# Gated delta rule of an encoder layer: 16-row blocks inverted by substitution, one block per partition, in place of three doubling levels

## The chip, the cores and the metric

The kernel runs on one core of one Trainium2 chip. TensorE is called PE here, VectorE DVE, ScalarE ACT, GpSimd POOL and SyncE SP. The metric is the device time of one execution in microseconds (us); of several executions the median counts.

## The reference

One layer of an encoder over 2048 tokens of width 1024, all in float32: an input projection, two groups of heads (gated delta rule and latent attention), an output projection, a feed-forward network and a gated embedding, with norms between. Only the delta rule concerns this change. For each of 4 heads (key and value width 128) and each chunk of 64 tokens:

```python
g = jnp.cumsum(chunks(g), axis=-1)
decay = jnp.exp(jnp.where(tri_incl, g[..., :, None] - g[..., None, :], -jnp.inf))
k_beta = k * beta[..., None]
lower = jnp.where(tri_strict, jnp.einsum('nbhid,nbhjd->nbhij', k_beta, k) * decay, 0.0)
rhs = jnp.concatenate([v * beta[..., None], k_beta * jnp.exp(g)[..., None]], -1)
sol = lax.linalg.triangular_solve(lower + jnp.eye(CHUNK), rhs, left_side=True, lower=True, unit_diagonal=True)
u, w = sol[..., :DV], sol[..., DV:]
attn = jnp.where(tri_incl, jnp.einsum('nbhid,nbhjd->nbhij', q, k) * decay, 0.0)
...
v_new = u_c - jnp.einsum('bhck,bhkv->bhcv', w_c, state)
o = jnp.einsum('bhck,bhkv->bhcv', q_c, state) + jnp.einsum('bhij,bhjv->bhiv', attn_c, v_new)
state = state * jnp.exp(gl)[..., None, None] + jnp.einsum('bhck,bhcv->bhkv', k_c, v_new)
```

q and k are normed to length one per head beforehand; o gets a root-mean-square norm, a gain and a gate z.

## The kernel before

`build` (L2643) calls eight stages one after the other, each with its own buffers and semaphores and a barrier at its end: `project_in`, `latents`, `delta_rule`, `attention`, `project_norm`, `feed_in`, `project_norm`, `embed`. Stages exchange tensors through HBM. The change is in `delta_rule` (L625) alone, and in the two scratch tensors that `build` now makes for it.

`delta_rule` works on 16 tiles of 128 tokens, two chunks each, all four heads together, so most instructions work on 128 partitions by 512 elements (4 heads by 128). There are three jobs for a tile:

- **first**: load q, k, v (768 KB, names `dr_qkv`), transpose them on PE, take sums of squares on ACT (`p_squares`), roots and one Newton step (`p_newton`), scale q and k (`p_scale`, `dr_qk_n`), transpose them back (`p_back`), products of k with k and of q with k (`p_gram`), masks of decays on POOL (`masks`, `dr_dec`), from which DVE makes the triangle L (`p_grams`, L1232), whose transpose gives the first U (`p_turn_l`, `p_inverse`).
- **solve**: the inverse U of 1+L, by five doubling levels of sizes 2, 4, 8, 16, 32. A level is `s_z` on PE (transposes of U L939, products of L and U L941), a copy T on ACT (L1116), a masked copy Z on DVE (L1247), `s_y` on PE (L948) and a subtraction on DVE (`s_u`, L1252). Then `s_wu` makes w and u.
- **advance**: twice per tile, a chunk's step of the state S: `a_state` (L974, L978) and `a_update` (L986, L989) on PE, `a_v` (L1257) and `a_s` (L1268) on DVE, with a scaled state `Sd` from POOL (L853); then `a_squares`, `a_norm` (L1272 to L1279), a transpose `a_out` and `a_gate` (L1285), which writes `dr_mix`, stored by SP.

The order is written out by hand for each engine in a function `all_three`: one round holds the advance of tile t, the solve of tile t+1 and the first job of tile t+2, interleaved. `pipeline` runs 14 such rounds in hardware loops of two, with a filling round ahead and two emptying ones behind. Engines meet by semaphores only, and each engine takes its instructions strictly in the order written. SP's queue holds the loads of q, k, v (four tiles ahead, two buffers), of z, and the stores of `mix`.

Of the kernel before, what the change touches and what calls it, by code (L numbers as in the profile page):

```python
# [24 lines left out]
ACT = mybir.ActivationFunctionType  # L25
# [599 lines left out]
def delta_rule(nc, hT, a_log, dt_bias, norm_g, mixT):  # L625
# [5 lines left out]


    LEVELS = (2, 4, 8, 16, 32)
    BETA, GCUM, BETA_G, K_DEC, GATE = range(5)
    with ExitStack() as ctx:
        s = Scope(nc, ctx, "dr")
        qkv = s.sb("qkv", [P, 2, 3 * HEADS, P])
# [8 lines left out]
        cur = s.sb("cur", [P, 2, 5, HEADS])  # L646
# [5 lines left out]
        corner = s.sb("corner", [P, 1 + len(LEVELS), P])  # L652
        eps_l2 = s.sb("eps_l2", [P, 1])
        cums = s.sb("cums", [P, HEADS, P])
        eg = s.sb("eg", [P, 2, HEADS, P])
        e_last = s.sb("e_last", [P, HEADS, 2])
# [3 lines left out]
        qk_n = s.sb("qk_n", [P, 2 * HEADS, P])  # L660
        vb = s.sb("vb", [P, 2, HEADS, P])
        kbg = s.sb("kbg", [P, 2, HEADS, P])
        kdec = s.sb("kdec", [P, 2, HEADS, P])
        qk_nT = s.sb("qk_nT", [P, 2 * HEADS, P])
        dif = s.sb("dif", [P, HEADS, P])
        dec = s.sb("dec", [P, 2, HEADS, P])
        L = s.sb("L", [P, 2, HEADS, P])
        Z = s.sb("Z", [P, HEADS, P])
        Z0 = s.sb("Z0", [P, HEADS, P])
        U = s.sb("U", [P, 2, HEADS, P])  # L670
        T = s.sb("T", [P, HEADS, P])
        attnT = s.sb("attnT", [P, 2, HEADS, P])
        wT = s.sb("wT", [P, 2, HEADS, P])
        u = s.sb("u", [P, 2, HEADS, P])
        qdT = s.sb("qdT", [P, 2, HEADS, P])
        S = s.sb("S", [P, HEADS, P])
        Sd = s.sb("Sd", [P, HEADS, P])
# [5 lines left out]
        mix = s.sb("mix", [P, HEADS, P])  # L683
# [5 lines left out]
        loaded = [s.sem(f"loaded{b}") for b in range(2)]  # L689
        z_loaded = [s.sem(f"z_loaded{b}") for b in range(2)]  # L690
        cur_done = s.sem("cur_done")
        cums_done = s.sem("cums_done")
        qk_turned = s.sem("qk_turned")
        turned_done = s.sem("turned_done")
        eg_done = s.sem("eg_done")
        ssq_done, log_done, root_done = s.sem("ssq_done"), s.sem("log_done"), s.sem("root_done")
        newton = s.sem("newton")
        scaled = s.sem("scaled")
        vb_done = s.sem("vb_done")
        dif_done, dec_done = s.sem("dif_done"), s.sem("dec_done")  # L700
        kbg_done, kdec_done = s.sem("kbg_done"), s.sem("kdec_done")
        masked = s.sem("masked")
        back_done, back_copied = s.sem("back_done"), s.sem("back_copied")
        gram_done = s.sem("gram_done")
        L_done, attn_done = s.sem("L_done"), s.sem("attn_done")
        LT_done, z0_done, u_done = s.sem("LT_done"), s.sem("z0_done"), s.sem("u_done")

# [3 lines left out]
        qd_done = s.sem("qd_done")  # L711
        last_done = s.sem("last_done")
# [5 lines left out]
        NL = len(LEVELS)  # L718
        PAIR = [slice(0, 2), slice(2, 4)]
        solve_ps = [solve0, solve1]  # L720
        N_MASKS = 5 + 2 * (1 + NL) + 1
        PRE_GATE = 13

        def column(c):
# [1970 lines left out]
```

## Time and profile before

| what | us |
|---|---|
| median of 3 runs (3538.44 to 3544.13) | 3541.79 |
| the profiled execution, its own time | 3540.79 |
| its span, first to last instruction | 3539.3 |
| `delta_rule`: first mask instruction to the end of the last `dr_mix` | 705.4 to 1207.2 |

The page lists for each group of instructions the line, the engine, the operation, the names written and read, the count, the busy time, the mean duration of one, and the idle time of the engine ahead of them with what ended it. The timeline lists instructions in order of time: start, length, engine, line, and in brackets the idle time before and its releaser. A table by stretches gives, for each stretch from start to end, its length, the busy time and count for PE, PE's weight loads, DVE, ACT and POOL, then the granted PE clock as a share of 2.4 GHz, the share of the DMA engines' time and the GB/s. A float32 matmul counts as two instructions of PE, a transpose as one.

### The profile page before, as it was taken

Reading aid. Unit: us, or ns where it says so; the run is one execution under the profiler, and the core shown is the slowest. Engines: PE = TensorE matmul, PEld = TensorE weight load, DVE = VectorE, ACT = ScalarE, POOL = GpSimd, SP = SyncE. Lnnn points to the kernel's source line nnn. Section 1 sums busy time; section 2 is a strip of 40 time slices with the busy share of each in tenths; the row PEclk is TensorE's granted clock in tenths of the full one; section 3 lists DMA queues with packets and bytes.
Section 4 is the critical chain, followed back from the end, with each engine's and each line's share of the span. In section 5 each row is a group of like instructions: output and inputs, shape, how many; then the busy total and the mean of one; then the engine's idle time right before and its main releaser. Section 6 shows DMA issues by size and latency. Waiting matters only on the chain. (4 is left out here: it accounts for less than half of the span.)

```text
span 3539.3 us, 48206 instructions
## 1 busy us (share of the span) xinstructions
PE 3218.3 (91%) x16244; PEld 2679.7 (76%) x16244; DVE 1689.5 (48%) x2776; ACT 1131.5 (32%) x2514; POOL 1037.2 (29%) x863
## 2 busy tenths in 40 slices
PE   7999987779999689796997999989999799999798
PEld 5888864568888577685875888878888588888576
DVE  3652004346666555554567554585555433333433
ACT  2111014334444355454224333343333311111321
POOL 2222212033333176652006333363333100000222
PEclk9999998989999899998998999999999899999899
DMA  3212124311111311102553322212222533333433
GB/s 137 77 71 83 71 97 129 118 54 48 45 52 28 84 57 43 53 21 94 176 168 137 123 78 89 79 64 89 78 82 65 190 101 97 97 93 98 161 120 105
DMA packets 263069, 323.20 MB, mean 91 GB/s; under 512 B 15152, under 2 KB 205616, under 8 KB 258480
## 3 DMA queue, kind: packets, MB, share of 16 engines
q1 hardware_dynamic: 211544, 239.09, 21.2%
q0 software_dynamic: 18144, 66.07, 5.2%
q10 hardware_dynamic: 33280, 16.78, 1.7%
q8 instruction: 53, 0.87, 0.1%
q14 instruction: 48, 0.39, 0.0%
HBM read 209.68 MB, written 112.20 MB: 91 GB/s over the span
## 5 line engine op out<-in xcount | busy, mean ns | idle before, releaser
L1942 PE MATMUL ff_bank<-ff_x_hi,ff_w_lo 128*128 128x512 f32 x1240 | 489.1, 394 | 34.3 <-DVE ff_w_lo L2122 19.7
L1943 PE MATMUL ff_bank<-ff_x_lo,ff_w_hi 128*128 128x512 f32 x1240 | 488.0, 394 | 0.0
L1944 PE MATMUL ff_bank<-ff_x_hi,ff_w_hi 128*128 128x512 f32 x1240 | 487.6, 393 | 0.0
L1925 POOL TENSOR_TENSOR ff_w_sum<-ff_w_raw 128x512 f32<-128x512 f32 x210 | 294.3, 1411 | 504.3 <-DVE ff_w_lo L2122 443.3
L1942 PEld LDWEIGHTS ff_bank<-ff_x_hi,ff_w_lo 128*128 128x128 f32 x1240 | 236.0, 190 | 86.7 <-DVE ff_w_lo L2122 22.8
L2322 PE MATMUL fd_acc<-fd_w_hi,fd_a_lo 128*128 128x512 f32 x704 | 278.0, 395 | 25.4 <-DVE fd_a_lo L2306 25.4
L176 PE MATMUL in_h_ps<-in_x_hi,in_w_lo 128*128 128x512 f32 x704 | 276.8, 393 | 25.5 <-POOL in_w_lo L153 25.5
L177 PE MATMUL in_h_ps<-in_x_lo,in_w_hi 128*128 128x512 f32 x704 | 276.2, 392 | 0.0
L178 PE MATMUL in_h_ps<-in_x_hi,in_w_hi 128*128 128x512 f32 x704 | 276.2, 392 | 0.0
L2324 PE MATMUL fd_acc<-fd_w_hi,fd_a_hi 128*128 128x512 f32 x704 | 275.8, 392 | 0.0
L2323 PE MATMUL fd_acc<-fd_w_lo,fd_a_hi 128*128 128x512 f32 x704 | 275.8, 392 | 0.0
L1944 PEld LDWEIGHTS ff_bank<-ff_x_hi,ff_w_hi 128*128 128x128 f32 x1240 | 236.1, 190 | 49.5
L1943 PEld LDWEIGHTS ff_bank<-ff_x_lo,ff_w_hi 128*128 128x128 f32 x1240 | 236.1, 190 | 48.8
L2021 ACT ACTIVATE ff_w_hi<-ff_w_sum 128x512 fp32r<-128x512 f32 x210 | 132.6, 631 | 285.7 <-PE ff_bank L1944 266.3
L2306 DVE TENSOR_TENSOR fd_a_lo<-fd_a_raw,fd_a_hi 128x256 fp32r<-128x256 f32 x176 | 74.6, 424 | 277.8 <-ACT fd_a_hi L2296 277.8
L2296 ACT ACTIVATE fd_a_hi<-fd_a_raw 128x256 fp32r<-128x256 f32 x176 | 73.1, 416 | 346.3 <-PE fd_acc L2324 338.7
L1502 POOL TENSOR_TENSOR at_prob<-at_prob,at_scale 128x512 f32<-128x512 f32 (+4 forms) x112 | 133.6, 1223 | 158.6 <-DVE at_scale L1688 98.9
L2322 PEld LDWEIGHTS fd_acc<-fd_w_hi,fd_a_lo 128*128 128x128 f32 x704 | 133.2, 189 | 56.2 <-DVE fd_w_lo L2303 26.6
L176 PEld LDWEIGHTS in_h_ps<-in_x_hi,in_w_lo 128*128 128x128 f32 x704 | 133.5, 190 | 54.4 <-issue 17.3
L178 PEld LDWEIGHTS in_h_ps<-in_x_hi,in_w_hi 128*128 128x128 f32 x704 | 133.4, 189 | 28.0
L177 PEld LDWEIGHTS in_h_ps<-in_x_lo,in_w_hi 128*128 128x128 f32 x704 | 133.5, 190 | 27.7
L2324 PEld LDWEIGHTS fd_acc<-fd_w_hi,fd_a_hi 128*128 128x128 f32 x704 | 133.1, 189 | 28.0
(368 smaller groups left out, 6858.4 us busy)
## 6 DMA issues: line engine op xcount, KB each, us to landing
ff_w_raw<-w_gate_up SPq DMA_DIRECT2D x44, 1024.0 KB, 5.2
scratch_hT<-in_out SPq DMA_DIRECT2D x22, 1024.0 KB, 3.8
fd_a_raw<-scratch_hid SPq DMA_DIRECT2D x176, 128.0 KB, 2.1
dr_qkv<-scratch_hT SPq DMA_DIRECT2D x16, 768.0 KB, 5.0
in_w_raw<-w_in POOLq DMA_DIRECT2D x22, 512.0 KB, 3.8
scratch_hid<-ff_first SPq DMA_DIRECT2D x44, 256.0 KB, 2.3
scratch_hid<-ff_second SPq DMA_DIRECT2D x44, 256.0 KB, 2.3
in_x_raw<-xT SPq DMA_DIRECT2D x8, 1024.0 KB, 4.8
```

Source lines behind the costliest of these rows:

```text
L176: pe.matmul(acc, w_lo[:, b, ws], x_hi[:, k, ts], start=(k == 0), stop=False)
L177: pe.matmul(acc, w_hi[:, b, ws], x_lo[:, k, ts], start=False, stop=False)
L178: last = pe.matmul(acc, w_hi[:, b, ws], x_hi[:, k, ts], start=False, stop=(k == KD - 1))
L1502: op = pool.tensor_tensor(view, view, by, ALU.mult)
L1925: pool.tensor_tensor(w_sum[:, SUM_SLOT[m]], w_raw[:, b, one], w_raw[:, b, two], op).then_inc(w_sum_done, 1)
L1942: pe.matmul(acc, w_lo[:, wm, ws], x_hi[:, xm, k], start=first_mm, stop=False, skip_group_check=skip)
L1943: pe.matmul(acc, w_hi[:, wm, ws], x_lo[:, xm, k], start=False, stop=False, skip_group_check=skip)
L1944: return pe.matmul(acc, w_hi[:, wm, ws], x_hi[:, xm, k], start=False, stop=last_mm, skip_group_check=skip)
L2021: act.activation(w_hi[:, m], src, ACT.Copy).then_inc(w_hi_done, 1)
L2322: pe.matmul(to, self.a_lo[:, slot, rows], self.w_hi[:, k, cols], start=(k == k0), stop=False)
L2323: pe.matmul(to, self.a_hi[:, slot, rows], self.w_lo[:, k, cols], start=False, stop=False)
L2324: last = pe.matmul(to, self.a_hi[:, slot, rows], self.w_hi[:, k, cols], start=False, stop=(k == k1))
```

## The change

`delta_rule` is written anew. The parts, in words:

- **No norming of q and k.** The products are made from `dr_qkv` as loaded; the norms go into factors per row (`p_factors`, `made`, `rnq`). `p_scale`, `p_back`, both copies back and the transposes of L are gone. `kdec` and `kbg` move from POOL to DVE, the state's scaling joins DVE's addition (four instructions of one head each in place of one on POOL and one on DVE).
- **Blocks of 16 rows.** Levels 2, 4 and 8 (and the size-1 start) are gone. Instead SP stores L to HBM (256 KB), loads its 32 diagonal blocks of 16 by 16 back with one block in each of 32 partitions (four loads of 128 pieces of 64 bytes), POOL inverts them in 29 instructions (`substitute`), SP stores the result (32 KB), loads it back spread over 128 partitions (512 pieces of 64 bytes), and DVE puts the blocks on U's diagonal (`spread`). Levels 16 and 32 stay.
- **Four tiles in flight.** A round r holds the first job of tile r, the substitution of tile r-1, the solve of r-2 and the advance of r-3. There are 19 rounds, written out without hardware loops. Buffers grow: `qkv` 3, `eg`, `kdec`, `attnT`, `qdT` 4, `L`, `kbg`, `vb` 3, `mix` 2.

```diff
-    LEVELS = (2, 4, 8, 16, 32)
+    BASE = 16
+    NB = P // BASE
+    LEVELS = (16, 32)
...
+            for r in range(TILES + 3):
+                m, e, n, t = (x if 0 <= x < TILES else None for x in (r, r - 1, r - 2, r - 3))
+                yield m, e, n, t
...
+            for m, e, n, t in steps():
+                if e is not None:
+                    sp.wait_ge(inv_step, INV * (e + 1))
+                    sp.dma_start(blocks_U[e], inv[:, e % 2].rearrange("p j i -> p (j i)")).then_inc(inv_stored, 16)
+                    if e + 3 < TILES:
...
+                        load(e + 3)
+                    sp.wait_ge(inv_stored, 16 * (e + 1))
+                    reached(sp, u_done, e - 1)
+                    src = blocks_U[e].rearrange("(h r) (j i) -> (r j) h i", h=HEADS, j=BASE)
+                    sp.dma_start(u_blk[:, e % 2], src).then_inc(u_loaded[e % 2], 16)
+                if m is not None:
+                    sp.wait_ge(L_done, m + 1)
+                    sp.dma_start(blocks_L[m], L[:, m % 3].rearrange("p h f -> p (h f)")).then_inc(L_stored, 16)
+                    sp.wait_ge(L_stored, 16 * (m + 1))
+                    reached(sp, inv_step, INV * (m - 1))
+                    row = HEADS * P
+                    for h in range(HEADS):
+                        src = bass.AP(blocks_L.tensor, blocks_L[m].offset + h * P,
+                                      [[BASE * row + BASE, NB], [row, BASE], [1, BASE]])
+                        sp.dma_start(blk[h * NB:(h + 1) * NB, m % 2], src).then_inc(blk_loaded[m % 2], 16)
...
+            def substitute(e):
...
+                pool.wait_ge(blk_loaded[b], 16 * HEADS * (e // 2 + 1))
+                reached(pool, inv_stored, 16 * (e - 1))
+                low = blk[:, b].rearrange("p i j -> p j i")
+                pool.tensor_tensor(inv[:, b], ident_b[:], low, ALU.subtract).then_inc(inv_step, 1)
+                for k in range(1, BASE - 1):
+                    shape = [HEADS * NB, k, BASE - 1 - k]
+                    by = blk[:, b, k + 1:, k].unsqueeze(1).broadcast_to(shape)
+                    row = inv[:, b, 0:k, k:k + 1].broadcast_to(shape)
+                    to = part[:, 0:shape[1] * shape[2]].rearrange("p (j i) -> p j i", j=k)
+                    rest = inv[:, b, 0:k, k + 1:]
+                    pool.wait_ge(inv_step, n + 2 * k - 1)
+                    pool.tensor_tensor(to, by, row, ALU.mult).then_inc(inv_step, 1)
+                    pool.wait_ge(inv_step, n + 2 * k)
+                    pool.tensor_tensor(rest, rest, to, ALU.subtract).then_inc(inv_step, 1)
...
+            for m, e, n, t in steps():
+                if m is not None:
+                    sums(m)
+                if e is not None:
+                    substitute(e)
+                if m is not None:
+                    decayed(m)
+                    masks(m)
...
+            def p_lower(m):
+                dve.wait_ge(gram_done, m + 1)
+                dve.wait_ge(masked, 3 * m + 3)
...
+                dve.tensor_tensor(L[:, m % 3], b0[:], dec[:, 0], ALU.mult).then_inc(L_done, 1)
...
+            def spread(e):
+
+                shape = [P, HEADS, NB, BASE]
+                dve.wait_ge(u_loaded[e % 2], 16 * (e // 2 + 1))
...
+                dve.tensor_tensor(U[:, e % 2].rearrange("p h (r i) -> p h r i", i=BASE),
+                                  u_blk[:, e % 2].unsqueeze(2).broadcast_to(shape),
+                                  diag[:].rearrange("p (r i) -> p r i", i=BASE).unsqueeze(1).broadcast_to(shape),
+                                  ALU.mult).then_inc(u_done, 1)
```

The order on POOL, one round in the middle of the stage, before (`dr_Sd` is the scaled state, `dr_dec` the masks):

```order
L826 TENSOR_TENSOR dr_cums<-dr_upto,dr_cur 128x512
L85 REGISTER_ALU
L853 TENSOR_TENSOR dr_Sd<-dr_S,dr_e_last 128x512
L852 REGISTER_ALU
L853 TENSOR_TENSOR dr_Sd<-dr_S,dr_e_last 128x512
L831 TENSOR_TENSOR dr_dec<-dr_dif,dr_below 128x512
```

and now, the end of the substitution of tile r-1 (`dr_part` and `dr_inv`; 24 rows of the same kind stand ahead of these) and what follows it for tile r:

```order
L843 TENSOR_TENSOR dr_part<-dr_blk,dr_inv 32x26
L845 TENSOR_TENSOR dr_inv<-dr_inv,dr_part 32x13x2
L843 TENSOR_TENSOR dr_part<-dr_blk,dr_inv 32x14
L845 TENSOR_TENSOR dr_inv<-dr_inv,dr_part 32x14
L860 TENSOR_TENSOR dr_qdT<-dr_qkv,dr_eg 128x512
L850 TENSOR_TENSOR dr_dec<-dr_dif,dr_upto 128x512
L852 TENSOR_TENSOR dr_dec<-dr_dif,dr_below 128x512
L855 TENSOR_TENSOR dr_dec<-dr_dec,dr_made 128x512
L827 TENSOR_TENSOR dr_cums<-dr_upto,dr_scal 128x512
```

The masks of tile r stand behind the whole substitution of tile r-1, where before only two scalings of the state stood ahead of them.

The order on SP's queue, one round in the middle of the stage, before:

```order
L752 DMA dr_qkv<-scratch_hT 128x12x128
L763 REGISTER_ALU
L764 ISA
L764 DMA scratch_mixT<-dr_mix 128x4x128
L756 ISA
L756 DMA dr_zT<-scratch_hT 128x4x128
```

and now (`blocks_L` and `blocks_U` are the new scratch tensors in HBM):

```order
L762 DMA scratch_blocks_U<-dr_inv 32x256
L745 DMA dr_qkv<-scratch_hT 128x12x128
L771 DMA dr_u_blk<-scratch_blocks_U 128x4x16
L774 DMA scratch_blocks_L<-dr_L 128x512
L781 DMA dr_blk<-scratch_blocks_L 8x16x16 x4
L785 DMA scratch_mixT<-dr_mix 128x4x128
L749 DMA dr_zT<-scratch_hT 128x4x128
```

The load of q, k, v now stands between the store of the inverted blocks and their load back, and L's store and the blocks' loads follow on the same queue.

The order on DVE, the end of a round, before (from the norm of the output to the end of the round):

```order
L1279 TENSOR_TENSOR dr_on<-dr_b,dr_orn 128x512
L1252 TENSOR_TENSOR dr_U<-dr_U,dr_b 128x256 x2
L1228 ISA
L85 ISA
L1232 TENSOR_TENSOR dr_L<-dr_b,dr_dec 128x512
L1246 REGISTER_ALU
L1247 TENSOR_TENSOR dr_Z<-dr_b,dr_corner 128x256 x2
L1235 TENSOR_TENSOR dr_attnT<-dr_b,dr_dec 128x512
L1252 TENSOR_TENSOR dr_U<-dr_U,dr_b 128x256 x2
```

and now:

```order
L1206 TENSOR_TENSOR dr_U<-dr_u_blk,dr_diag 128x512
L1243 TENSOR_TENSOR dr_orn<-dr_orn 128x4
L1244 TENSOR_SCALAR dr_ossq<-dr_ossq 128x4
L1246 TENSOR_TENSOR dr_orn<-dr_orn,dr_ossq 128x4
L1248 SCALAR_TENSOR_TENSOR dr_orn<-dr_orn 128x4
L1250 TENSOR_TENSOR dr_orn<-dr_orn,dr_rnq 128x4
L1253 TENSOR_TENSOR dr_on<-dr_b,dr_orn 128x512
L1193 TENSOR_TENSOR dr_L<-dr_b,dr_dec 128x512
L1198 TENSOR_TENSOR dr_attnT<-dr_b,dr_dec 128x512
L1259 SCALAR_TENSOR_TENSOR dr_mix<-dr_b,dr_gnorm,dr_zT 128x512
```

L of tile r now stands behind the instruction that reads the loaded blocks of tile r-1 (L1206) and behind the norm of tile r-3.

## Rows read from the trace of the kernel before

**Rows 1.** Busy time by stretch: us, busy per engine, clock, DMA, GB/s.
```profile
786.40:1190.00 403.60, 397.21 (x3164) 357.11 (x3162) 257.01 (x590) 182.11 (x728) 131.22 (x119) 1.00 0.14 40
```

**Rows 2.** The same view, one steady tile.
```profile
977.71:1006.48 28.77, 28.36 (x229) 25.52 (x227) 18.38 (x43) 13.44 (x55) 9.94 (x10) 1.00 0.16 46
```

**Rows 3.** Timeline, POOL's first mask in two tiles: start, us, engine, line.
```profile
977.71 1.27 POOL L831 TENSOR_TENSOR dr_dec<-dr_dif,dr_below 128x512 f32<-128x512 f32 x1 [2.02 <-ACT dr_dif L1098]
...
1006.48 1.27 POOL L831 TENSOR_TENSOR dr_dec<-dr_dif,dr_below 128x512 f32<-128x512 f32 x1 [2.02 <-ACT dr_dif L1098]
```

**Rows 4.** Timeline of PE in that tile: a level, then transposes back.
```profile
978.08 1.16 PE L948 MATMUL dr_b<-dr_Z,dr_T 128*128 128x128 f32 x8
...
979.31 0.44 PE L939 MATMUL dr_b<-dr_ident,dr_U 128*128 128x128 f32 x2
...
980.79 1.16 PE L986 MATMUL dr_b<-dr_vnew,dr_kdec 64*128 64x128 f32 x8
...
982.93 1.09 PE L879 MATMUL dr_b<-dr_ident,dr_qk_n 128*128 128x128 f32 x8
```

**Rows 5.** Groups by shape, POOL: count, busy us, mean ns, idle before.
```profile
L1502 POOL TENSOR_TENSOR at_prob<-at_prob,at_scale 128x512 f32<-128x512 f32 x32 | 33.1, 1040 | 23.7 <-DVE at_scale L1688 23.7
...
L1502 POOL TENSOR_TENSOR at_prob<-at_prob,at_scale 128x128 f32<-128x128 f32 x16 | 6.4, 400 | 44.7 <-DVE at_scale L1668 44.7
...
L834 POOL TENSOR_TENSOR dr_dec<-dr_dif,dr_upto 128x512 f32<-128x512 f32 x16 | 20.4, 1275 | 0.0
...
L804 POOL MEMSET dr_eps_l<- 128x1 f32 x1 | 0.1, 98 | 0.0
```

**Rows 6.** The timeline of POOL and SP in the stage's set-up.
```profile
705.76 0.66 SPq L771 DMA_DIRECT2D dr_bias<-dt_bias  x1
...
706.47 0.42 SPq L772 DMA_DIRECT2D dr_rate<-a_log  x1
...
706.93 0.43 SPq L773 DMA_DIRECT2D dr_gnorm<-gdn_norm_g  x1
...
708.43 0.66 POOL L798 TENSOR_SCALAR_AFFINE_SELECT dr_corner<-dr_ones 128x64 f32<-128x64 f32 x1
...
713.13 0.25 POOL L798 TENSOR_SCALAR_AFFINE_SELECT dr_corner<-dr_ones 128x64 f32<-128x64 f32 x1
...
713.44 0.24 POOL L798 TENSOR_SCALAR_AFFINE_SELECT dr_corner<-dr_corner 128x64 f32<-128x64 f32 x1
```

**Rows 7.** DMA issues by line: size of each, median us from issue to landing.
```profile
dr_qkv<-scratch_hT SPq DMA_DIRECT2D x16, 768.0 KB, 5.0
...
scratch_mixT<-dr_mix SPq DMA_DIRECT2D x16, 256.0 KB, 2.4
...
scratch_mixT<-at_out SPq DMA_DIRECT2D x32, 128.0 KB, 1.9
...
dr_bias<-dt_bias SPq DMA_DIRECT2D x1, 2.0 KB, 2.5
```

**Rows 8.** The view of one tensor, zT: last line, all its loads.
```profile
DMA to landing us min/median/max: 2.8/2.8/8.0
```

**Rows 9.** The timeline of the last tile, and the first tile's L.
```profile
1194.06 1.06 PE L974 MATMUL dr_b<-dr_S,dr_wT 128*64 128x128 f32 x8 [0.79 <-issue]
...
1203.86 0.16 DVE L1272 TENSOR_TENSOR dr_orn<-dr_orn 128x4 f32<-128x4 f32 x1 [1.99 <-ACT dr_orn L1135]
...
1204.53 0.69 DVE L1279 TENSOR_TENSOR dr_on<-dr_b,dr_orn 128x512 f32<-128x512 f32 x1
...
1206.42 0.75 DVE L1285 SCALAR_TENSOR_TENSOR dr_mix<-dr_b,dr_gnorm,dr_zT 128x512 f32<-128x512 f32 x1 [1.21 <-PE dr_b L879]
...
736.46 0.69 DVE L1232 TENSOR_TENSOR dr_L<-dr_b,dr_dec 128x512 f32<-128x512 f32 x1 [6.90 <-PE dr_b L920]
```

**Rows 10.** PE around a long idle, then the clock of that stretch.
```profile
751.19 1.97 PE L879 MATMUL dr_b<-dr_ident,dr_qk_n 128*128 128x128 f32 x8 [3.42 <-DVE dr_qk_n L1224]
...
752.00:756.00 4.00, 4.00 (x21) 4.00 (x20) 0.84 (x2) 1.09 (x2) 1.92 (x2) 0.50 0.00 0
```

More of the change, by code:

```diff
@@ L773, in _ @@
             sp.dma_start(gnorm[:], norm_g).then_inc(small_loaded, 16)
[L774 removed]
+            for t in range(3):
+                load(t)
             for t in range(2):
[L776 to L784 removed]
@@ L813, in _ @@
             put(below[:], chunk[:], ALU.is_gt, 0.0, 0, [[-1, P]], 1)
[L814 removed]
+            for l, size in enumerate(LEVELS):
                 blocks = P // (2 * size)
@@ L864, in all_three @@
-            def all_three(t, b, has_first=True, has_advance=True):
-                if has_first:
-                    sums(t + 2, b)
-                if has_advance:
-                    advance(t, b)
-                if has_first:
-                    masks(t + 2, b)
-                    products(t + 2, b)
-            pipeline(first, advance, all_three)(pool.Fori)
+            by_block = lambda ap: ap.rearrange("p (n r) -> p n r", r=BASE)
+            put(by_block(diag[:]), by_block(ones[:]), ALU.is_ge, 0.0, 0, [[-BASE, NB], [0, BASE]], 1)
@@ L875, in _, with transposes @@
         @block.tensor
         def _(pe):
-            def transposes(out, src, n0, count):
-                for h in range(count):
+            def transposes(out, src, n0):
+                for h in range(HEADS):
                     last = pe.transpose(out[:, h], src[:, n0 + h], ident[:])
@@ L1340, in _ @@
-            pre_scalars()
-            pipeline(first, advance, all_three)(dve.Fori)
+                dve.wait_ge(z_loaded[t % 2], 16 * (t // 2 + 1))
+                reached(dve, stored[t % 2], 16 * (t // 2))
+                dve.scalar_tensor_tensor(mix[:, t % 2], b2[:], gnorm[:, 0:1], zT[:, t % 2], ALU.mult, ALU.mult).then_inc(mix_done, 1)
+            pre_scalars()
+            for m, e, n, t in steps():
+                first, base, solve, advance = (x is not None for x in (m, e, n, t))
+                if advance:
+                    a_v(t, 0)
+                if solve:
+                    s_z(n, 0)
+                if advance:
+                    a_s(t, 0)
+                    a_v(t, 1)
+                if solve:
+                    s_u(n, 0)
+                if advance:
+                    a_s(t, 1)
+                if first:
+                    p_kdec(m)
+                    p_newton(m)
+                    p_factors(m)
+                    p_kbg(m)
+                if solve:
+                    s_z(n, 1)
+                    s_u(n, 1)
+                if base:
+                    spread(e)
+                if advance:
+                    a_norm(t)
+                if first:
+                    p_lower(m)
+                    p_attention(m)
+                if advance:
+                    a_gate(t)
```

700 lines of the change are left out of this document (297 added, 403 removed).

## The prediction

> **What bounds the kernel now.** I read the table by stretches first, to find the stage and who is busy in it. In the steady part of `delta_rule`, 403.6 us, PE is busy for 397.2 of it at the full clock of 2.4 GHz (share 1.00) [rows 1]. DVE has 257, ACT 182, POOL 131. Then one round: POOL's first mask starts at 977.71 and again at 1006.48, so a tile takes **28.77 us** [rows 3], of which PE is busy 28.36, DVE 18.4, ACT 13.4, POOL 9.9 [rows 2]. So the stage is bound by PE's work, 14 rounds of 28.8 us, with about 60 us of filling and emptying. The other stages are not touched: the whole change is what becomes of the time from 720 to 1207.2, where the last `dr_mix` ends [rows 9].
>
> **PE's side of the change.** A level's `s_y` starts at 978.08, its `s_z` at 979.31, the next group at 980.79: 2.71 us, of which I count some 0.25 between the two as waiting: 2.45 of work [rows 4]. Three levels go: 7.3 us. The eight transposes back are listed with 1.09 us, 0.9 without the overlap at their end, and four transposes of L with half of it [rows 4]. So 28.4 - 7.3 - 0.9 - 0.5 = **19.7 us of PE work** for a tile. The pieces left wait for one another somewhat more (a state step has the vector instruction between its two products, and fewer level pieces stand between); I put 2 us on it, so PE alone would allow a round of about 22. DVE: the levels' Z and U go, `kdec`, `kbg`, the spread and small factors come, the sum stays under 18.4. ACT loses copies. If nothing else entered, 14 rounds would each be 6.7 us shorter, 94 us in all. The question is what the new chain allows.
>
> **The new chain, step by step.** I follow it from the end of DVE's L of tile r to the end of L of tile r+1; both in the same place of a round, so this is the round's length if the chain binds. It is a closed loop, since SP, POOL and DVE each take their instructions in order: L(r) must go to HBM and back before POOL can substitute, and the masks and L of tile r+1 stand behind that on POOL and on DVE. The deeper buffers don't open this loop.
>
> 1. SP picks up (0.1 us, an estimate) and stores L, 256 KB. `mix` of the same size lands in 2.4 us [rows 7]. At 2.5.
> 2. Four loads of 64-byte pieces. SP issued small DMAs 0.71 and 0.46 us apart [rows 6]; three spacings of 0.5 and a landing of 2.5 for the last, as the broadcast of 128 small pieces took [rows 7], plus a pick-up: 4.1. At 6.6, POOL starts at 6.7.
> 3. `substitute`. POOL took 400 ns for 128 elements and 1040 for 512 with one broadcast operand [rows 5]: 1.67 ns for an element, 187 ns fixed; with two full operands 1275 for 512, 2.1 ns an element. The 28 small instructions have 14 to 56 elements, 40 in the mean (560 for each of two kinds, by 14): 0.26 us. A dependent instruction started 0.06 us behind its predecessor's end (713.13 + 0.25 to 713.44), I take 0.07. Short runs: 64 runs of one element took 0.66 us where two runs of 32 took 0.25 [rows 6], 6.6 ns a run for another kind of instruction; with 7.5 runs in the mean I take half of it, 0.025. So 28 x 0.355 = 9.9, and 0.8 for the first (256 elements): **10.7 us**. At 17.4. Bounds: below, every small one as cheap as the fill of one element, 0.098 [rows 5], plus the gap: 28 x 0.17 + 0.7 = 5.5; above, 0.400 as the nearest full row, plus gap and runs: 28 x 0.47 + 0.8 = 14.0. I stay between, since the line through the rows has them at 0.26.
> 4. The inverse is stored, 32 KB: 128 KB took 1.9, 256 KB 2.4 [rows 7]; 2.1 with a pick-up of 0.1. At 19.6. Meanwhile SP issues the next load of q, k, v at about 17.9; such a load lands after 5.0 us [rows 7], so at 22.9.
> 5. The blocks come back, issued at 19.7. Alone they would land after 2.5, at 22.2. But they stand behind 768 KB in the same queue. One load of z, alone 2.8 us, took 8.0 when it was issued behind two such loads [rows 8]. I take 0.8 us behind the big load's end: at 23.7. Bounds: 22.2 without queueing, 24.7 if such small pieces took 5.0 in all, as long as the 768 KB load [rows 7].
> 6. DVE: the spread 0.7, five small instructions of the norm and the product `on`. Before, four small ones took 1203.86 to 1204.53, and `on` 0.69 [rows 9]: 0.87 + 0.69. Then L, 0.69 [rows 9]. With a pick-up: 3.0. **At 26.7.**
>
> The other branch from step 3 goes through POOL's four big instructions (`qdT` and both plain masks 1.27 each, the last 1.04 [rows 5]): 17.4 + 4.9 + 0.7 = 23.0. It ends earlier. PE's branch ends at about 22. So the queue branch sets the round: 26.7 against 28.8. What PE saved is then mostly idle time: about 5 us of each round.
>
> [...]
>
> **Both ends of the stage.** The mask set-up has 12 instructions instead of 18, at 0.24 to 0.66 each [rows 6], about 2.5 us less. The first L ends at 737.15 [rows 9]; without scaling, transposes back and copies the first tile saves about another 4.7 us: 730. Then 15 rounds to L(15): rounds 1 and 2 have no norm (1.5 less each), rounds 14 and 15 no load in the queue (1.5 less each), so 4 x 25.2 + 11 x 26.7 = 394.5, at 1124.5. Then the last blocks (23), norm and gate of tile 13 (3): 1150.5. A round with only solve and advance: two levels 4.9, two state steps about 8, w and u with copies 3.3, some waits: 17. The last advance took 13.1 us before (1194.06 to 1207.17 [rows 9]); the output product now stands ahead of the second state product, 14.5. Cold PE, below: 3. End at 1185, against 1207.2: **22 us less**. The profiled execution had 3540.8, 1 us under the median, which is within the runs' spread: 3541.8 - 22 = **3520 us**. One us on the round is 14 us of the time. Idle PE costs speed when it comes back: after 3.42 us idle the eight transposes took 1.97 us instead of 1.09, and the clock was 0.50, the 1.2 GHz level, for the next 4 us [rows 10, 4]. With 5 us idle in each round the first 4 us of PE's work would take some 3 us longer; 22 + 3 = 25 is still under 26.7, so hidden, but the cover is only 1.7 us.
>
> **Rivals.**
> - **The chain is shorter, PE binds** (20%). POOL's small instructions cost under 0.29 us, or the queueing of step 5 isn't there (-1.5). The round then falls to 22 to 25: 3455 to 3496. For: the fill of one element takes 0.098. Against: nothing that reads two operands was seen that short.
> - **POOL's small instructions are dear; slower** (25%). At 0.42 us each, 0.065 more than taken, the round is 28.5 and the gain is gone; at 0.47 it is 30.0 and the time 3520 + 46 = 3566. Dearer 64-byte pieces (two loads on the chain, 1 us each) do the same. From a round of 28.6 the kernel is slower by over 0.2%. For: 64 short runs took 0.66. The place to see it is `substitute`.
> - **A wash** (12%): the same chain at 27.6 to 28.6, by 0.03 to 0.06 us per small instruction, 3535 to 3549.
> - **PE's clock opens the loop again** (3%): the first part of each round at 1.2 GHz makes PE's branch longer than the chain, 29 and more, 3555. Against: 25 by the rows above, and a shorter idle heals itself. The Trainium skill, "TensorE: Matmul & The Clock Gate", section "HAM oscillation", has PE return to the slow level after idle stretches between bursts; rows 10 show it once.
> - **Forecast** (40%): the queue branch binds at 25.2 to 27.6, 3499 to 3534.
>
> **How the numbers follow.** 0.2% of this kernel, 7 us, is about what a measurement can tell from no change. Faster: 40 + 20 and a little of the rest, 0.61. Same 0.12, slower 0.27. The range takes in the cheap case down to a round of 22.7 (3464) and the dear one up to 30.5 (3573).
>
> **What would show it.** Distance between two `dr_L` 26.7 us; `substitute` 10.7 us from first to last; DVE's instruction L1206 waiting for the DMA of `dr_u_blk`, not for POOL; PE busy about 20 of each 27 us, with one idle stretch before the output's transposes, and a clock under 1.00 in the steady part. Wrong if the masks (POOL) release L, if PE has no such gap, or if `dr_u_blk` lands in 2.5 us behind the load.

## The result, and the profile after

The changed kernel takes **3491.5 us** (median of 4 runs, 3487.7 to 3493.2) against 3541.5 before (3538.4 to 3544.1): ratio 0.9855, 95% interval 0.9841 to 0.9868. It is faster by 50 us, where 22 had been forecast. The direction and the chain that binds were as predicted, the size of the gain was not: the transfers on the chain land sooner than the prediction took. The profiled execution has a span of 3490.0 us, against 3539.3 before.

The table by stretches, in the steady part of `delta_rule` (columns as in [rows 1]):

```profile
778.30:1062.40 284.10, 245.43 (x1775) 212.56 (x1775) 152.05 (x440) 120.47 (x531) 162.88 (x404) 0.92 0.25 66
972.29:995.95 23.66, 21.11 (x154) 18.37 (x154) 12.94 (x39) 10.52 (x46) 13.98 (x34) 0.93 0.27 72
```

The second line is nearly one round. PE is busy for 86% of the stretch where it had 98% [rows 1], and its clock is 0.92 where it had 1.00. A round, from one `dr_L` to the next, takes 22.4 to 26.1 us, 24.13 in the mean of all 15; before, the round of [rows 3] took 28.8. The stage's last `mix` starts at 1149.4, where it had 1206.4 [rows 9].

I follow the loop of the prediction from L at 972.29 to L at 996.20, on three engines. The timeline of VectorE (start, duration, both in us):

```profile
972.29 0.68 DVE L1193 TENSOR_TENSOR dr_L<-dr_b,dr_dec 128x512 f32<-128x512 f32 x1
...
994.12 0.69 DVE L1206 TENSOR_TENSOR dr_U<-dr_u_blk,dr_diag 128x512 f32<-128x512 f32 x1 [3.50 <-DMA dr_u_blk<-scratch_blocks_U]
...
995.59 0.69 DVE L1253 TENSOR_TENSOR dr_on<-dr_b,dr_orn 128x512 f32<-128x512 f32 x1
996.20 0.68 DVE L1193 TENSOR_TENSOR dr_L<-dr_b,dr_dec 128x512 f32<-128x512 f32 x1
```

The same stretch on SyncE, whose rows are the issues of DMAs: L's store, the four loads of its blocks, the inverses' store, the next tile's load, the load of the inverses.

```profile
973.00 0.33 SPq L774 DMA_DIRECT2D scratch_blocks_L<-dr_L  x1
975.02 1.40 SPq L781 DMA_DIRECT2D dr_blk<-scratch_blocks_L  x4
...
988.42 0.33 SPq L762 DMA_DIRECT2D scratch_blocks_U<-dr_inv  x1
988.86 0.37 SPq L745 DMA_DIRECT2D dr_qkv<-scratch_hT  x1
989.91 0.36 SPq L771 DMA_DIRECT2D dr_u_blk<-scratch_blocks_U  x1
```

And GpSimd's start of the substitution in it:

```profile
977.94 0.84 POOL L835 TENSOR_TENSOR dr_inv<-dr_ident_b,dr_blk 32x256 f32<-32x256 f32 x1 [7.60 <-DMA dr_blk<-scratch_blocks_L]
```

Each step waits for the one before it: L ends at 972.97, the store is issued 0.03 later and is done when SyncE issues the block loads, at 975.02; POOL starts at 977.94; the inverses are stored from 988.42; the blocks are asked for at 989.91 and spread at 994.12; L starts 2.08 later. The groups of this stage by line (busy us, mean ns of one, idle time before them and what ended it):

```profile
L843 POOL TENSOR_TENSOR dr_part<-dr_blk,dr_inv 32x14 f32<-32x14 f32 (+6 forms) x224 | 61.0, 272 | 17.5
L845 POOL TENSOR_TENSOR dr_inv<-dr_inv,dr_part 32x14 f32<-32x14 f32 (+6 forms) x224 | 57.9, 258 | 17.6
...
L835 POOL TENSOR_TENSOR dr_inv<-dr_ident_b,dr_blk 32x256 f32<-32x256 f32 x16 | 13.5, 847 | 123.0 <-DMA dr_blk<-scratch_blocks_L 123.0
L1206 DVE TENSOR_TENSOR dr_U<-dr_u_blk,dr_diag 128x512 f32<-128x512 f32 x16 | 11.7, 731 | 79.2 <-DMA dr_u_blk<-scratch_blocks_U 79.2
L1193 DVE TENSOR_TENSOR dr_L<-dr_b,dr_dec 128x512 f32<-128x512 f32 x16 | 10.9, 682 | 4.7 <-POOL dr_dec L855 4.7
```

VectorE waits 79.2 us for the DMA of `dr_u_blk`, in all 16 tiles, and 4.7 us in all for the masks. PE pays for it at the end of the round, and then once more (timeline of PE):

```profile
967.92 1.06 PE L917 MATMUL dr_b<-dr_qkv 128*128 128x128 f32 x8
972.43 0.66 PE L876 MATMUL dr_b<-dr_ident,dr_on 128*128 128x128 f32 x4 [3.45 <-DVE dr_on L1253]
973.02 1.93 PE L959 MATMUL dr_b<-dr_S,dr_wT 128*64 128x128 f32 x8
```

It idles 3.45 us for `on` (2.5 to 4.8 us in most rounds), and the eight products behind that take 1.93 us, where they take 1.06 at the full clock [rows 9].

**Six long rounds.** Of the 16 stores of L ten land after 2.0 to 2.2 us, one after 2.4, five after 3.5 to 4.1. The view of the DMA queues, first in the 4.7 us around a slow store, then in the 2.3 us around a quick one (packets, MB, share of the stretch; then issues with KB and us to landing). The stretches differ in length, so the packets can be compared and the shares can't:

```profile
q1 hardware_dynamic: 144, 0.26, 15.2%
q8 instruction: 1, 0.02, 2.2%
...
scratch_blocks_L<-dr_L SPq DMA_DIRECT2D x1, 256.0 KB, 3.7
```

```profile
q1 hardware_dynamic: 144, 0.26, 29.9%
...
scratch_blocks_L<-dr_L SPq DMA_DIRECT2D x1, 256.0 KB, 2.0
```

In the 4.5 us from each of the 16 stores on, all five late stores have a packet of queue 8, whose kind is "instruction" (16 KB), and so has one quick store, that of the second tile, whose packet starts only 2.2 us after the store has landed. The one with 2.4 has a packet of queue 14 of that kind, and so has the first (2.2). The other eight, all at 2.0, have neither.

The packets themselves show more. A quick store has moved all its 144 packets 1.7 us after its issue. In each of the five late stores 135 have started within 1.9 us, and the last nine, one in sixteen, start only when the packet of queue 8 ends (the first of them 3 to 16 ns before its end). The landing waits for these nine. The same holds over the twelve kernels in which L is stored, the changed one and those of the experiments, 192 stores: of the 33 with a packet of queue 8 that starts within 2 us of their issue, 31 land after 2.6 to 4.1 us; of the 126 with no instruction packet in those 2 us, 125 land after 2.0 and one after 3.2. So such a packet, by its kind a fetch of code, holds up a sixteenth of the store. That this sixteenth is the share of one of the 16 DMA engines fits, but the trace doesn't name the engine of a packet, and no run changed the fetches. The five cost 8.4 us over 2.03 each. In the whole program queue 8 has 65 such packets, 53 before.

### The profile page after: what moved, and what is told of

The parts are those of the page before. It is cut to its first block and busy times, and to the rows that moved or that the text cites. A ratio compares the mean times of both kernels' runs of the same rounds, so it can differ in the third digit from the quotient of the medians.

```text
span 3490.0 us, 45608 instructions
## 1 busy us (share of the span) xinstructions
PE 3099.3 (89%) x15092; PEld 2561.5 (73%) x15092; DVE 1608.0 (46%) x2712; ACT 1085.7 (31%) x2386; POOL 1099.6 (32%) x1259
## 3 DMA queue, kind: packets, MB, share of 16 engines
q1 hardware_dynamic: 231768, 244.86, 22.4%
q8 instruction: 65, 1.06, 0.1%
## 5 line engine op out<-in xcount | busy, mean ns | idle before, releaser
L2337 POOL DMA_DIRECT2D scratch_x<-fd_y x16 | 8.5, 534 | 474.4 <-DVE fd_y L2437 474.4
```

## Experiments

All ratios are to the kernel before, measured beside each kernel on the same chip. "Distance" is the mean time from one `dr_L` to the next.

**1. The pipeline without the blocks.** All of the new pipeline stays, but the levels 2, 4 and 8 are on TensorE again, in an order that I wrote, interleaved with the state steps. The store of L, the substitution and the load back are gone. U starts as the identity, so the level of size 1 is left out.

```
-    LEVELS = (16, 32)
+    LEVELS = (2, 4, 8, 16, 32)
...
-                    substitute(e)
...
+                dve.tensor_copy(U[:, e % 2], each(ident[:])).then_inc(u_done, 1)
```

> Edit: the new pipeline, without norming and with its deeper buffers, but the inverse by five doubling levels 2 to 32 as before; no store of L, no blocks, no substitution. The size-1 start is left out: U starts as the identity, so part of the computation is missing (one transpose and two DVE instructions for a tile). Theory A (before, PE's work bound the stage, and three levels of 2.45 us each are what the change took off it): PE's work is 19.7 + 7.3 = 27.0 us a tile, distance of two L 27 to 28, time 3530 to 3545, about that of the kernel before. Rival (the gain comes from dropping the norming's transposes and from the deeper buffers): distance 25 or less, time under 3510.

Measured: 3568.0 us, ratio 1.0078 (1.0060 to 1.0096), so *slower* than before, and outside what I expected. From the fourth on, rounds take 29.9 to 31.2 us. The table by stretches, then a wait (us in total, times, longest):

```profile
800.00:1100.00 300.00, 273.32 (x2093) 242.68 (x2092) 196.23 (x494) 126.88 (x515) 58.14 (x50) 0.97 0.16 45
```

```profile
PEld dr_b L921 <- DVE dr_Z L1213: 17.4, 10, 1.7
```

PE has less work than before, but is busy for only 91% of the time. The state steps and five levels, in my order, wait for one another. Another order may do better, so the run does not show what the norming and its transposes are worth alone, only that leaving them out, in this order, is no gain. What it does show is PE's work: 273.32 us in 300, so 27.9 in a mean round of 30.6, where the pipeline with two levels and blocks has 19.6 (spread_half, experiment 4). The levels that go are 8 us of PE's work a round, and with the blocks in their place the pipeline is 76 us faster.

**2. Is it one closed chain?** The substitution cut to 7 of its 14 steps (edit below), and with each of its 28 small instructions issued twice. The first leaves out half of the steps, the second applies each one twice.

```
-                for k in range(1, BASE - 1):
+                for k in range(1, 7 + 1):
```

> The changed kernel with the substitution cut from 14 steps to 7, so that its inverses, and the output, are wrong: 14 of the 29 GpSimd instructions of a tile are left out, some 5.2 us of the 10.5 that the substitution takes in the trace after the change. A (one closed chain of 24.1 us a round sets the pace, until the TensorE work of a round does): the distance of two L falls from 24.1 to TensorE's own round. That is 22.6 us, as where the loads and the spreading were moved (TensorE busy about 20.2, 2.4 waiting for the gated output): 16 rounds less 1.5 each, 3467 us. B (the GpSimd chain does not bind at all, and the time goes elsewhere): the distance stays at 24.1 and the time at 3491. C (the chain alone binds, TensorE has slack): 18.9 a round, 3408.

> The changed kernel with each of the 28 instructions of the 14 substitution steps issued twice (the inverses are wrong by it): about 9.7 us more GpSimd work a round in the chain from L to the next L but one. A (closed chain, its parts in series): the distance goes from 24.1 by nearly the whole 9.7 to 33.5 to 34 us; 16 rounds of it, 3640 to 3650 us, and VectorE's wait for the inverted blocks grows by as much. B (the chain has slack elsewhere, TensorE sets the pace): below 29 a round, under 3570.

Doubled: 3637.2 us, ratio 1.0266 (1.0247 to 1.0284). The substitution takes 20.1 us instead of 10.5 and an undisturbed round 33.4 instead of 23.8: all 9.6 us arrive. Busy time by stretch, then the wait of the spreading (which has another line number here):

```profile
850.00:1200.00 350.00, 213.42 (x1540) 184.15 (x1540) 135.71 (x384) 105.14 (x460) 221.74 (x635) 0.80 0.18 49
```

```profile
L1210 DVE TENSOR_TENSOR dr_U<-dr_u_blk,dr_diag 128x512 f32<-128x512 f32 x11 | 7.8, 705 | 144.3 <-DMA dr_u_blk<-scratch_blocks_U 144.3
```

PE is busy for 61% at a clock of 0.80, and itself waits for the chain in every round. The closed chain (A) is shown: the distance is within its 33.5 to 34, the time 3 us under its 3640 to 3650. Halved: 3424.4 us, 0.9668 (0.9651 to 0.9685), 67 us faster than the changed kernel. The substitution falls by 4.9 us, the usual distance by 3.2, to 20.6. That is between my A (22.6) and C (18.9), and refutes B. My A was wrong on what TensorE's own round is: PE is busy for 207.5 of 220 us there, so the chain no longer has the round to itself. Experiment 4 gives the floor.

**3. The two obvious cuts of the chain.** *load_late*: SyncE issues the 768 KB load behind the four block loads, so that the inverses have the queue to themselves. *spread_late*: VectorE spreads the blocks behind L and the scores. *both_moves*: the load late and the spreading last in the round. The edit of spread_late:

```
-                if base:
-                    spread(e)
                 if advance:
                     a_norm(t)
                 if first:
                     p_lower(m)
                     p_attention(m)
+                if base:
+                    spread(e)
```

> Edit: the 768 KB load of q, k, v is moved on SP's queue from ahead of the load of the inverted blocks (dr_u_blk) to behind the loads of L's blocks. Theory A (the round is a closed chain through SP, POOL and DVE, and the blocks coming back queue behind the big load): the wait from the issue of dr_u_blk to DVE's spread falls from 4.2 us to 1.9, as in the two rounds of the changed kernel that have no load; the distance of two L falls from 24.1 to about 21.9 in the 13 rounds with a load, the time from 3491 to 3461. Theory B (PE's own work of 20 to 22 us binds already, the waits on DVE are slack): the distance stays at 23.5 or more, the time over 3482. Theory C (small pieces are slow whatever stands ahead of them): dr_u_blk still lands after 4 us.

> Edit: on DVE the spread of the inverted blocks is moved from ahead of the output's norm and L to behind L and attnT of the same round; the queue's order stays. Theory A: L no longer waits for the blocks of the tile before; what is late next is POOL's masks, which end 4.9 us behind the substitution, so L comes 2.9 us earlier in each round, distance about 21.3, time 3448. PE's idle stretch ahead of the output's transposes shrinks from 3.9 us to under 1.5 and the clock in the steady part rises from 0.91 to 0.97 or more. Theory B (PE binds): distance 23.5 or more, time over 3482.

> Edit: both moves together, with the spread as the last instruction of DVE's round. Theory A: only the branch through POOL is left: store of L 2.0, loads of its blocks 2.7, substitution 10.5, four big instructions of POOL 4.9, L 0.7: a distance of 20.8 us if PE (19.7 us of work) allows it, time 3440; with PE's waits 22, time 3459. Theory B: over 3482.

| kernel | median us | ratio to before, interval | distance |
|---|---|---|---|
| changed kernel | 3491.5 | 0.9855 (0.9841 to 0.9868) | 24.1 |
| load_late | 3478.1 | 0.9826 (0.9809 to 0.9842) | 23.1 |
| spread_late | 3465.3 | 0.9785 (0.9768 to 0.9802) | 22.9 |
| both_moves | 3467.0 | 0.9795 (0.9779 to 0.9812) | 23.05 |

Each move is a gain, but pays less than its size: theory A had 3461, 3448 and 3440, and is 17, 17 and 27 us off. Together the moves pay no more than the better one. In load_late the spreading starts 1.87 us (median) after the issue instead of 4.2, as expected, but from the spreading to L it now takes 3.7 us instead of 2.08. The timeline of VectorE there:

```profile
976.79 0.72 DVE L1206 TENSOR_TENSOR dr_U<-dr_u_blk,dr_diag 128x512 f32<-128x512 f32 x1 [1.06 <-DMA dr_u_blk<-scratch_blocks_U]
977.44 0.99 DVE L1243 TENSOR_TENSOR dr_orn<-dr_orn 128x4 f32<-128x4 f32 x1
978.36 0.16 DVE L1244 TENSOR_SCALAR dr_ossq<-dr_ossq 128x4 f32<-128x4 f32 x1
978.55 0.88 DVE L1246 TENSOR_TENSOR dr_orn<-dr_orn,dr_ossq 128x4 f32<-128x4 f32 x1
...
980.47 0.68 DVE L1193 TENSOR_TENSOR dr_L<-dr_b,dr_dec 128x512 f32<-128x512 f32 x1
```

Two operations on 128x4 elements take 0.99 and 0.88 us, where the group of L1243 has a mean of 208 ns and that of L1246 of 164 ns in the changed kernel. The norming, started earlier, runs into GpSimd's big products. In spread_late the coincidence can be read to the hundredth. First VectorE, then GpSimd, at the same time:

```profile
1001.60 1.00 DVE L1246 TENSOR_TENSOR dr_orn<-dr_orn,dr_ossq 128x4 f32<-128x4 f32 x1
1002.63 0.96 DVE L1248 SCALAR_TENSOR_TENSOR dr_orn<-dr_orn 128x4 f32<-128x4 f32 x1
...
1004.43 0.68 DVE L1193 TENSOR_TENSOR dr_L<-dr_b,dr_dec 128x512 f32<-128x512 f32 x1
```

```profile
1001.54 1.04 POOL L855 TENSOR_TENSOR dr_dec<-dr_dec,dr_made 128x512 f32<-128x512 f32 x1
1002.54 1.04 POOL L827 TENSOR_TENSOR dr_cums<-dr_upto,dr_scal 128x512 f32<-128x512 f32 x1
```

The two small ones end at 1002.60 and 1003.59; GpSimd's two end at 1002.58 and 1003.58. Each small one waits until GpSimd's has ended. It isn't a coincidence of one round. In all 14 traces together the norming's operations with both inputs in SBUF run 880 times. 144 of them take over 0.25 us, and every one of these ends 0.01 to 0.03 us behind a 128x512 product of GpSimd; none of the 736 short ones runs inside a GpSimd instruction. The longest, in spread_late, sits through three products that follow each other without a pause, 954.37 to 958.07:

```profile
954.36 3.74 DVE L1250 TENSOR_TENSOR dr_orn<-dr_orn,dr_rnq 128x4 f32<-128x4 f32 x1
```

The Trainium skill, "SBUF — State Buffer", section "SBUF: two separate sides", has a port pair that VectorE and GpSimd share. An operation holds it for the whole of its length, and the Trainium skill counts VectorE's operations with two inputs in SBUF among those that need it, against a GpSimd operation that reads SBUF. These rows agree. The one-input L1244 stays at 0.16 in the rows above, but once in spread_late it too was held, for 1.31 us, until GpSimd's product ended.

So L is released by the norming, and the masks end only 1.85 us before it. I saw here PE's wait for `on`, 1.3 to 3.2 us in nearly every round, and took that for the new bound.

**4. Who binds at 22.6?** On spread_late: *out_late* moves the output's transposes and its gating into the next round (so PE needn't wait for `on`), *spread_half* halves the substitution. TensorE's part of out_late's edit:

```
+                    if t:
+                        a_out(t - 1, m - 1 if first else None)
...
-                if advance:
-                    a_out(t, m)
+            a_out(TILES - 1, None)
```

> The kernel of spread_late, and the transposes of the gated output and their gating (a_out, a_gate) moved from the end of a round into the next one: on TensorE behind the first a_kv, on VectorE behind the second a_v. In spread_late TensorE waits 2.0 to 2.4 us a round for the normed output before these transposes, and runs the next 1 to 2 us at the lower clock. A (with the chain of blocks out of the way, TensorE's own round with this wait is the bound): the distance falls from 22.6 to 20.2 to 20.7 and the time by 16 times 2.0 to 2.4, to 3427 to 3435. B (the chain through the blocks is as late as the wait is: 22 us or so): the distance falls by 0.6 at most, the time is 3455 to 3465, and TensorE waits elsewhere, for L or for the spread blocks.

> The kernel of spread_late with the substitution cut to 7 of 14 steps (the inverses are wrong by it), so 5.2 us less GpSimd work a round. A (TensorE's round with its wait for the gated output binds there at 22.6): no change, distance 22.6 but for the few longer rounds in which the store of L is slow, which now have slack: 3455 to 3465. B (the chain through the blocks binds): 17.5 to 20 a round, 3390 to 3420.

out_late: 3465.4 us, 0.9786 (0.9769 to 0.9804), nothing gained; spread_half: 3416.2 us, 0.9640 (0.9623 to 0.9658), 49 us less. Both answers are B: the chain still binds, and PE's wait was slack, not cause. In out_late a wait of the same size stands at another place, ahead of the new tile's U (a line of the waits from 800 to 1030 us), and in spread_half PE is the bound (table by stretches):

```profile
PEld dr_b L930 <- DVE dr_U L1207: 24.0, 10, 3.6
```

```profile
800.00:1020.00 220.00, 213.28 (x1676) 183.75 (x1675) 159.22 (x415) 113.10 (x495) 111.44 (x219) 1.00 0.29 78
```

97% busy at a clock of 1.00, and 12 of the 15 distances are 20.2 us: **20.2 is TensorE's own round** with this order.

**5. The loop through the masks.** With the spreading behind L, the loop left is L, store, block loads, substitution, `qdT` and the masks, norming, L. *l_first* puts L ahead of the norming (on out_late), *l_masks* also puts the two products that L needs ahead of the two others on GpSimd, *l_masks_load* also has the late load. The edit of l_first against out_late:

```
-                if advance:
-                    a_norm(t)
                 if first:
                     p_lower(m)
                     p_attention(m)
                 if base:
                     spread(e)
+                if advance:
+                    a_norm(t)
```

> The kernel of out_late with VectorE's order changed once more: L, the decayed scores and the spreading now ahead of the norming of the output (a_norm), where they stood behind it. In spread_late VectorE ran the norming from 1001.15 to 1004.5, of which 1.96 us were two 128x4 operations of 1.00 and 0.96 us, and L began at 1004.43, while GpSimd had finished its masks at 1002.58. A (the loop L, store, load, substitution, masks, norming, L is the bound, and the norming was its last part): the distance falls by 1.85 from 22.6 to 20.7, the time by 25 to 30 us to 3435 to 3440. B (TensorE's round is the bound, whatever VectorE's order): the distance stays at 22.5, 3460 to 3467.

> The kernel of l_first, and on GpSimd the order behind the substitution changed: the two products that L needs first (1.26 and 1.04 us), then that of the scores, then the decayed queries (1.26 us each), where the last two stood ahead of them. A (the same loop, now 2.5 us shorter): the loop comes to 2.03 + 2.7 + 10.5 + 2.3 + 0.9 = 18.4, below TensorE's round, so TensorE's round of about 20 binds: distance 20.0 to 20.3, 3415 to 3425, and the rounds with a slow store of L are lengthened by less. B (the loop through the inverted blocks, spread at L + 21 us and needed at the start of the next round, is late next): the distance stays at about 20.7, 3435, and TensorE waits for U of the spreading.

> The kernel of l_masks, with the load of the next tile on SyncE's queue behind the 32-row block loads, as in load_late, so that the inverted blocks land 1.87 us after their issue and not 4.2. A (TensorE's round binds in l_masks already): the same within 3 us. B (the inverted blocks are late there, and TensorE waits for U): up to 2.3 us a round off the wait, distance to 19.7 to 20.2, 5 to 25 us faster than l_masks.

l_first: **3437.4 us**, 0.9699 (0.9683 to 0.9716), distance 21.2, usually 20.9: its A. The norming no longer meets GpSimd's products; its L1244 (L1243 before the edit) falls from 842 ns in spread_late to

```profile
L1244 DVE TENSOR_TENSOR dr_orn<-dr_orn 128x4 f32<-128x4 f32 x16 | 2.5, 158 | 3.6 <-ACT dr_orn L1106 3.6
```

l_masks: 3431.5 us, 0.9688 (0.9671 to 0.9704), distance 20.95; l_masks_load: 3430.4 us, 0.9680 (0.9664 to 0.9696), 20.6. l_masks can't be told from either of the others. l_first and l_masks_load, measured beside each other, are 7 us apart and their single times don't overlap (3432.5 to 3439.3, 3428.3 to 3431.0). I expected 20.0 to 20.3 in l_masks; most of its rounds stay at 20.8, and TensorE waits there for U, its B. In l_masks_load most rounds are 20.8 as well. Its time is within A's 3 us, and B's gain of 5 to 25 isn't there, but TensorE still waits for U: the inverted blocks now land in time, and the spreading comes late for another reason. The rows of l_masks_load, VectorE's end of a round and PE's start of the next, and its stretch:

```profile
974.62 0.69 DVE L1194 TENSOR_TENSOR dr_L<-dr_b,dr_dec 128x512 f32<-128x512 f32 x1 [3.15 <-PE dr_b L917]
975.23 0.68 DVE L1200 TENSOR_TENSOR dr_attnT<-dr_b,dr_dec 128x512 f32<-128x512 f32 x1
975.83 0.68 DVE L1208 TENSOR_TENSOR dr_U<-dr_u_blk,dr_diag 128x512 f32<-128x512 f32 x1
...
976.57 0.44 PE L930 MATMUL dr_b<-dr_ident,dr_U 128*128 128x128 f32 x2 [0.96 <-DVE dr_U L1208]
...
800.00:1020.00 220.00, 204.02 (x1629) 178.93 (x1627) 137.43 (x404) 112.60 (x487) 148.05 (x355) 1.00 0.29 79
```

VectorE's L now waits for PE's Gram product (the last `dr_b L917`); the scores and the spreading follow on VectorE; and PE waits for the spreading, by 0.96 us. The loop has become TensorE's round and VectorE's three instructions at its end. The clock is 1.00 again.

**6. The last wait.** l_masks_load with the spreading ahead of L again, where VectorE is idle for 3.15 us.

```
+                if base:
+                    spread(e)
                 if first:
                     p_lower(m)
                     p_attention(m)
-                if base:
-                    spread(e)
```

> The kernel of l_masks_load with one line moved: VectorE spreads the inverted blocks ahead of L again, where the changed kernel has it and where it stood in the way there. In l_masks_load the inverted blocks are asked for at 971.34 and land about 1.9 us later, at 973.3, while VectorE is idle from 971.5 until the last Gram product ends at 974.6; TensorE then waits 0.96 us a round for U. A (the place is free now: TensorE's round binds, and the blocks are there before the Gram product): that wait goes, distance 20.8 to 19.8 to 20.0, 16 rounds of 0.9, 3413 to 3420. B (the blocks come too late again, as in the changed kernel, or the loop through GpSimd of 18.4 to 19 us plus the landing closes at over 20.8): no change or slower, 3430 to 3445, and VectorE waits for dr_u_blk.

Measured: 3436.2 us, 0.9698 (0.9682 to 0.9714), by the medians 6 us slower than l_masks_load, with intervals that overlap: no gain, a miss for A, its B. The wait for U is gone in most rounds, but (VectorE, then PE, of one round):

```profile
973.61 0.69 DVE L1208 TENSOR_TENSOR dr_U<-dr_u_blk,dr_diag 128x512 f32<-128x512 f32 x1 [1.76 <-DMA dr_u_blk<-scratch_blocks_U]
975.00 0.69 DVE L1194 TENSOR_TENSOR dr_L<-dr_b,dr_dec 128x512 f32<-128x512 f32 x1 [0.70 <-PE dr_b L917]
```

```profile
978.48 1.16 PE L966 MATMUL dr_b<-dr_vnew,dr_kdec 64*128 64x128 f32 x8 [1.03 <-DVE dr_vnew L1230]
```

PE now waits 0.9 to 1.8 us for `vnew`, since VectorE still has the scores and the norming to do before it, and the chain seems to have no slack again (no run tried it): the distances go from 19.9 to 23.8, 21.3 in the mean, and long where the block loads came late (4.36 us after their issue in the longest). I had counted one wait and one landing, and left out what stands next in VectorE's queue.

## Why the prediction was right, and where its size was not

The mechanism was forecast and is there; three terms of the sum were too large, and so the time of 3491.5 us lies below the 3499 to 3534 forecast for this chain.

*The bound and its place: right.* The signs that name a place are there: VectorE's L1206 waits for the DMA and not for POOL, PE has one gap, ahead of the output's transposes, its clock is 0.92, and POOL's masks are not what releases L. The doubled substitution shows that the chain is closed. The set-up was right too: the first L ends 24.2 us after the stage's first instruction (at 730.9), with 24.6 forecast (730). The tail takes 57.3 us from the end of the last L, with 60.5 forecast.

*The length of the round: 24.1 and not 26.3 in the mean.* By the prediction's own steps, measured as medians, so for a round without a slow store:

| step | forecast | measured | difference |
|---|---|---|---|
| 1. store of L, with pick-up | 2.5 | 2.06 | -0.4 |
| 2. block loads, to POOL's start | 4.2 | 2.7 | -1.5 |
| 3. substitution | 10.7 | 10.5 | -0.2 |
| 4. inverses stored | 2.3 | 1.5 | -0.8 |
| 5. blocks back, behind 768 KB | 4.0 | 4.2 | +0.2 |
| 6. spread, norm, `on`, L | 3.0 | 2.76 | -0.2 |

**The terms that failed are the transfers of steps 1, 2 and 4**, sized too large by 2.7 us of a round together; that makes up most of the difference between the 22 us forecast and the 50 measured. For step 2 I had taken 2.5 us for a landing from a broadcast of 128 pieces [rows 7] and three spacings of 0.5 from the stage's set-up [rows 6]. Here the four are issued 0.35 apart, which is 0.5 of the 1.5 us, and POOL starts 1.3 us after the last issue is done (1.5 in the round above), which is the rest. For step 4 I went from 128 KB at 1.9 and 256 KB at 2.4 [rows 7] down to 2.1 for 32 KB, but 256 KB of L land in 2.0 and 32 KB in 1.5. Why the rows that I took are longer, by their layouts or by what else was moving, wasn't tried. The slow stores gave back 0.6 us a round in the mean.

*The terms that held.* The biggest and most doubtful one, the 28 small instructions, was taken at 0.355 us from start to start; it is 0.345 (10.5 less 0.85 for the first, over 28). The timeline of POOL:

```profile
954.96 0.21 POOL L843 TENSOR_TENSOR dr_part<-dr_blk,dr_inv 32x14 f32<-32x14 f32 x1
...
959.34 0.29 POOL L845 TENSOR_TENSOR dr_inv<-dr_inv,dr_part 32x56 f32<-32x56 f32 x1
959.71 0.30 POOL L843 TENSOR_TENSOR dr_part<-dr_blk,dr_inv 32x56 f32<-32x56 f32 x1
```

From 14 to 56 elements it costs 0.21 to 0.30 us, some 2 ns an element and 0.18 fixed. The gap between two is 0.08 throughout. The queueing of step 5 was taken too small (1.5, measured 2.35: 4.2 with the load ahead, 1.87 in the rounds without one), but on a landing taken too large (2.5), so their sum held by luck: two errors cancel.

*PE's own round* was put at 22, 19.7 of work and 2 of waits; in spread_half it is 20.2, with 19.6 of work. The work was right, and its pieces wait for one another some 1.5 us less than I took. That mattered only for the rival "PE binds", whose range holds the measured time, though by neither of its reasons: the small instructions cost what I had said, and the queueing is there. The others fall: POOL's instructions are not dear, the round is not at 27.6, and the clock's fall stays hidden behind the chain. It costs PE some 1.5 us a round, where 3 had been taken: 21.1 us busy in the round at 972.29, at a clock of 0.93, and 19.6 in spread_half's, at 1.00.

*The sum.* The last L ends at 1092.8 instead of 1124.5 and the stage at 1150.1 instead of 1185: 57 us less than before, 35 of them more than forecast. But the whole is only 49 us shorter. From the end of the stage to the end of the program it takes 2339.9 us where it took 2332.1, with the same instructions. "The other stages are not touched" holds for the code, not for the time. I looked at this rest in all profiled executions: 2333.3 (levels_back), 2333.7 (half_subst), 2335.4 to 2337.8 in seven, 2338.4 to 2340.2 in three, the changed kernel 2339.9, and before lowest with 2332.1. It doesn't follow the length of the stage. The stage's start moves too, from 701.6 to 706.7 (705.4 before, 706.7 in the changed kernel), with the same code ahead of it. So 8 us of an untouched rest change from kernel to kernel; why wasn't settled, and one profile of each doesn't say how steady it is. Had the rest stayed at 2332.1, the gain would have been 57. A difference of some 5 us between two of these kernels can lie outside the stage.

## What to carry to other kernels

When work leaves the bounding engine for a detour over other engines and HBM, ask first whether the detour is a *loop* through in-order queues; its length, not the engines' load, sets the round, and the gain is what the loop leaves. That deeper buffers don't open it is argued from the order alone, no run varied them; that the order in the queues does is shown: five moves of whole instructions in VectorE's, GpSimd's, TensorE's and SyncE's order were worth another 61 us (3491 to 3430), more than the rewriting itself had brought, though one of them alone (out_late) gained nothing. After each cut, follow the chain anew: an engine that waits each round, as PE did for `on`, may only have slack, and a thing moved earlier may meet another engine there.

## What the runs showed of the chip

- GpSimd: `tensor_tensor` on 32 partitions with 14 to 56 elements takes 0.21 to 0.30 us (medians by size), and a dependent one starts 0.08 after it; with 256 elements it takes 0.85.
- VectorE's small operations with two inputs in SBUF take 0.16 us alone. While GpSimd runs a 128x512 product they end with it: 1.0 us behind one, up to 3.7 behind three in a row.
- Landings: 256 KB to HBM 2.0 us, 32 KB 1.5; small blocks back 1.87 alone, 4.2 when issued 1.05 us behind 768 KB.
- The 256 KB store of L lands after 2.0 us when nothing is beside it. Where a 16 KB packet of queue 8's instruction kind starts within 2 us of its issue, it lands after 2.6 to 4.1 in 31 of 33 cases; in the five of the changed kernel nine of the store's 144 packets start only when that packet ends. Unrolled code, of which there is more in this kernel (65 such packets, 53 before), can so cost time in data transfers.
- PE after 3.45 us idle: eight products 1.93 us instead of 1.06; with its longest waits down to some 1 us (l_masks_load), the steady part of the stage runs at a clock of 1.00.
